# The first two sums of seven-product MLP units, written by an accumulating DMA instead of a VectorE add

## The reference

```python
m = rms_norm(h, mlp_norm[i])
h = h + jnp.square(jax.nn.relu(m @ w_mlp_up[i])) @ w_mlp_down[i]
```

## Time and profile before

| | us |
|---|---|
| median of 3 runs | 1630.5 |
| lowest and highest run | 1630.49, 1630.96 |
| span of the profiled execution | 1630.0 |
| TensorE busy | 1623.6 |
| VectorE busy | 1017.8 |
| ScalarE busy | 660.2 |
| GpSimd busy | 115.0 |

### The profile page before, as it was taken

How to read it: one execution, slowest core, us unless ns; L and a number is a source line. 1 busy time by engine, 2 the same in 40 slices (tenths; PEclk the granted TensorE clock), 3 DMA queues, 4 the chain that set the end, 5 groups by cost and what they waited for, 6 DMA issues and landing times.

```text
span 1630.0 us, 20189 instructions
## 1 busy us (share of the span) xinstructions
PE 1623.6 (100%) x8480; PEld 1345.9 (83%) x8480; DVE 1017.8 (62%) x1523; ACT 660.2 (41%) x919; POOL 115.0 (7%) x102
## 2 busy tenths in 40 slices
PE   9999999999999999999999999999999999999999
PEld 7877878898989888888888888877777888888887
DVE  6797664696756757576466357546655576366353
ACT  5476445354444446333122223456565333122221
POOL 1300000011111100000000000312101100000000
PEclk9999999999999999999999999999999999999999
DMA  5310228356454521222322313322221223222211
GB/s 187 109 46 27 104 78 121 82 115 136 87 135 86 161 84 72 79 102 104 107 100 100 107 59 124 101 94 87 76 77 52 78 104 111 98 102 98 109 59 71
DMA packets 28059, 156.01 MB, mean 96 GB/s; under 512 B 3712, under 2 KB 5392, under 8 KB 12096
## 3 DMA queue, kind: packets, MB, share of 16 engines
q1 hardware_dynamic: 26352, 149.75, 25.7%
q0 software_dynamic: 1328, 4.86, 5.5%
q10 hardware_dynamic: 288, 0.10, 0.0%
HBM read 149.98 MB, written 4.72 MB: 95 GB/s over the span
## 4 chain that ended last, share of the span: by engine, by line
PE 94%; DVE 3%; ACT 2%; DMA 1%; POOL 0%; issue 0%; SPq 0%; DVEq 0%; ACTq 0%
PE bank L725 23%; PE bank L726 23%; PE bank L727 23%; PE bank L731 3%; PE bank L733 3%; PE bank L732 3%; PE bank L1183 2%; PE bank L1185 2%; PE bank L1184 2%; PE bank L1421 1%; PE bank L980 1%; PE bank L1431 1%; PE bank L1447 1%; ACT WH L1490 1%; DMA RAW<-in_W 1%; PE bank L965 1%
## 5 line engine op out<-in xcount | busy, mean ns | idle before, releaser
L1913 DVE TENSOR_TENSOR WL<-RAW,WH 128x2048 fp32r<-128x2048 f32 (+2 forms) x122 | 273.0, 2243 | 193.5 <-ACT WH L1490 193.5
L725 PE MATMUL bank<-AH,WH 128*128 128x512 f32 (+1 forms) x974 | 382.9, 393 | 0.6 <-DVE WL L1963 0.4
L727 PE MATMUL bank<-AH,WL 128*128 128x512 f32 (+1 forms) x974 | 379.2, 389 | 0.0
L726 PE MATMUL bank<-AL,WH 128*128 128x512 f32 (+1 forms) x974 | 379.1, 389 | 0.0
L1490 ACT ACTIVATE WH<-RAW 128x2048 fp32r<-128x2048 f32 (+2 forms) x122 | 227.0, 1867 | 174.3 <-PE bank L727 138.0
L725 PE MATMUL bank<-HH,WH 128*128 128x512 f32 x608 | 236.6, 389 | 0.0
L726 PE MATMUL bank<-HL,WH 128*128 128x512 f32 x608 | 236.6, 389 | 0.0
L727 PE MATMUL bank<-HH,WL 128*128 128x512 f32 x608 | 236.5, 389 | 0.0
L725 PEld LDWEIGHTS bank<-AH,WH 128*128 128x128 f32 (+1 forms) x974 | 182.5, 187 | 42.4 <-issue 2.4
L727 PEld LDWEIGHTS bank<-AH,WL 128*128 128x128 f32 (+1 forms) x974 | 182.4, 187 | 38.7
L726 PEld LDWEIGHTS bank<-AL,WH 128*128 128x128 f32 (+1 forms) x974 | 182.5, 187 | 38.3 <-issue 1.0
(11 more groups left out here) (347 smaller groups left out, 2378.9 us busy)
## 6 DMA issues: line engine op xcount, KB each, us to landing
RAW<-in_W SPq DMA_DIRECT2D x124, 1024.0 KB, 4.8
RAW<-in_W SPq DMA_DIRECT2D x9, 768.0 KB, 4.2
X<-in_XT SPq DMA_DIRECT2D x16, 256.0 KB, 5.4
ev_scratch<-ev POOLq DMA_DIRECT2D x16, 160.0 KB, 7.6
Gb<-ev_scratch SPq DMA_DIRECT2D x16, 128.0 KB, 3.0
Gb<-ev_scratch SPq DMA_DIRECT2D x16, 112.0 KB, 2.7
out<-X SPq DMA_DIRECT2D x7, 256.0 KB, 2.0
RAW<-in_W SPq DMA_DIRECT2D x2, 512.0 KB, 5.6
```

The lines of the kernel that those rows point to most:

```text
L725: e.matmul(o, a, h, start=first, stop=False)
L726: e.matmul(o, a, l, start=False, stop=False)
L727: return e.matmul(o, c, h, start=False, stop=last)
L1913: e.tensor_tensor(k.WL[j][:, 0:n], k.RAW[RAW_OF[u]][:, 0:n], k.WH[j][:, 0:n].bitcast(F), SUB).then_inc(*WLO.mark(u))
```

## The change

Seven of the eleven fast units (up7, 8, 9, 11, 12, 13, 15: all but up5, and but the second of each run) no longer make "s1" on VectorE. SP writes block 3 of the unit's weights twice into `stage[0:2]`, from memory, once stageB of the fast unit before has been split, and adds 16 to `sums_seeded`. POOL waits for that and issues a DMA that adds blocks 0 and 1, again read from memory, to `stage[0:2]`; its landing adds 16 to `sums_added`. VectorE waits for this and goes on with "s2" and "s4". POOL's issue stands at "mid" of the unit two before, or, for up9 and up13, at the first down step of the group of four ahead. SP's seed stands right behind the unit's own load.

```diff
+def fast_before(u):
+
+    return max((v for v in FAST if v < u), default=0)
+
+
+SEEDED = [u for u in sorted(FAST) if fast_before(u) and (u - 1 not in FAST or u - 2 in FAST)]
...
+    k.seeded, k.summed = semaphore("sums_seeded"), semaphore("sums_added")
...
     def added(u):
 
         raw = k.RAW[RAW_OF[u]][:, :].rearrange("p (c n) -> p c n", c=4)
-        before = max((v for v in FAST if v < u), default=0)
-        w.wait_ge(loaded(k, u), WLO("stageB", before) if before else DVE("tl", 3))
-        e.tensor_tensor(k.stage[:, 0:2, :], raw[:, 0:2, :], raw[:, 3:4, :].to_broadcast([P, 2, QUARTER]), ADD).then_inc(
-            *DVE.mark("s1", u))
-        w.wait_ge(DVE("s1", u))
+        before = fast_before(u)
+        if u in SEEDED:
+            w.wait_ge(loaded(k, u), (k.summed, 16 * (SEEDED.index(u) + 1)))
+        else:
+            w.wait_ge(loaded(k, u), WLO("stageB", before) if before else DVE("tl", 3))
+            e.tensor_tensor(k.stage[:, 0:2, :], raw[:, 0:2, :], raw[:, 3:4, :].to_broadcast([P, 2, QUARTER]), ADD).then_inc(
+                *DVE.mark("s1", u))
+            w.wait_ge(DVE("s1", u))
...
+    def add_blocks(u):
+
+        w.wait_ge((k.seeded, 16 * (SEEDED.index(u) + 1)))
+        e.dma_start(k.stage[:, 0:2, :], k.W[u, :, 0:2 * QUARTER].rearrange("p (i n) -> p i n", i=2), accum_op=ADD).then_inc(k.summed, 16)
+
     for step, *x in mlp_order():
+        if step == "mid" and x[0] + 2 in SEEDED:
+            add_blocks(x[0] + 2)
+        elif step == "down" and x[1] == 0 and UNIT["down", 4 * x[0] + 3] + 1 in SEEDED:
+            add_blocks(UNIT["down", 4 * x[0] + 3] + 1)
...
     for u in range(3, attention + 4):
         load(u)
+        if u in SEEDED:
+            w.wait_ge(WLO("stageB", fast_before(u)))
+            e.dma_start(k.stage[:, 0:2, :], k.W[u, :, None, 3 * QUARTER:4 * QUARTER].to_broadcast([P, 2, QUARTER])).then_inc(k.seeded, 16)
```

## The result

| | before | after |
|---|---|---|
| median of 3 runs, us | 1630.5 | 1666.1 |
| lowest and highest, us | 1630.49, 1630.96 | 1665.13, 1667.03 |
| span of the profiled execution, us | 1630.0 | 1663.3 |

The ratio is 1.0219, with a 95% interval of 1.0201 to 1.0238: 35.6 us slower. 1651.5 was forecast, with a range of 1639 to 1672.

What follows compares the result with a forecast made beforehand. TensorE, busy 1623.6 of 1630.0 us, was taken as the bound, so the adds were worth 0; loop stalls of 19.3 us plus 1.7 for the clock made 21.0: 1651.0 profiled, 1651.5 as a median, range 1639 to 1672.

Steps and rivals of the forecast that it cites:

- What bounds the kernel: TensorE, busy 1623.6 of 1630.0 us, never waits for VectorE; taking the adds off VectorE is worth 0.
- Rival 3: Faster: VectorE's 8.5 us less work would free TensorE somewhere; at best 1630 us, chance 0.02.
- The loop: Through one buffer, stage: D + 6.6 us per unit against TensorE's 9.84; stalls sum to 19.3 us.
- Rival 1: Quick transfers: both DMAs land in about 3.0 us, D near 6.0, 3.6 us lost, 1634; chance 0.08 of under 1639.
- D: Time from stageB of the unit before to the landing of the sums: 9.7 us, ends 7.7 and 12.9.
- 512 KB should land in 3.6: SP's seed of stage, sized by the slope between loads of 1024 and 768 KB: 3.6 us, at least 3.0.
- The accumulate without a load: POOL's accumulating DMA into stage: 4.6 us as pe_x plus 1.2 for the extra read, 5.8; bounds 4.6 and 9.0.
- Rival 2: Slow accumulate: at 12 us D = 15.9, stalls 50.3 us, time 1684; chance 0.10 of over 1672.
- VectorE's part of the loop: VectorE's steps from the end of the add to the end of stageB: 6.57 us, taken as 6.6.
- The clock term: TensorE falls to half clock at one of the long stalls (up8, up12): 1.7 us, ends 0 and 3.4.
- up9 and up13: At these units 14 us hide a load of 4.8 and a D of 9.7, so the stall is 0.
- The margin of 0.4 us behind up8: First down split comes 8.04 us behind stageB of up8, TensorE needs it after 8.43; loss 0, but not by much.

Runs made afterwards that it cites:

- e_no_add: The kernel before without the add of 128x1024 in all eleven units, nothing in its place (output wrong): 1630.3 us, ratio 1.0004.
- e_two_buffers: The kernel after with a second buffer for the first two sums of up7, up11 and up15, all DMA bytes kept: 1630.8 us, ratio 1.0004.
- e_filled: The kernel after with useless products ahead of product a of up7, 8, 11, 12 and 15, keeping TensorE busy: 1664.6 us.
- e_load_later: The kernel after with SP's load behind the seed (up7, 8, 11, 12, 15) held until the sums have landed: 1653.5 us, ratio 1.0142.
- e_plain_second: e_load_later with POOL's DMA as a plain copy instead of an accumulate: 1647.4 us in one run.
- e_load_first: The kernel after with SP's load of the next unit issued ahead of the seed (up7, 8, 11, 12, 15): 1659.4 us, ratio 1.0178.
- e_covered: The kernel after with only up9 and up13 seeded, the other five making their sums on VectorE: 1630.4 us, ratio 0.9998.
- e_wide_seed: e_load_later with the seed reading blocks 2 and 3 in runs of 4 KB (sums wrong): 1652.3 us in one run.
- e_scalar_seed: The kernel after with ScalarE seeding stage by a copy of block 3 from RAW instead of SP's DMA: 1640.2 us, ratio 1.0055.

## Why the prediction was right, and where its size was off

**What bounds the kernel** held: without the add, and without any DMA in its place, the time is the same (e_no_add, 0.9995 to 1.0013). Rival 3, faster, falls with it.

**The loop** held, in its place, its order and its formula: the same bytes outside the loop cost about 1.5 us (e_two_buffers), and TensorE waits in just up7, 8, 11, 12 and 15, released by VectorE. It does so at "a" in all five, but at "c" only in up11 and up15: in up7, 8 and 12, where the prediction had waits at both, "a" ran at half clock and ended just as stageB did. Rival 1, quick transfers, fell by the landings: 5.9 and 7.1 us, not 3.0. Even the plain copy of 512 KB with no load beside it took 4.1, from POOL's queue. The Trainium skill (DMA: Bandwidth & Descriptors, Anatomy of one DMA) has 2.0 us plus bytes over 436 GB/s, an estimate of 3.2 us for it; page and measurement differ, and the measurement decides. (The D = 6.7 of rival 1 took this estimate, which is for GpSimd's DMAs, for SP's seed as well.)

**D was mis-sized**, 9.7 instead of 13.3, worth 17.8 us, of which VectorE's part (below) took some 2.5 back; that is the gap between 21.0 and 35.6 us. The term "512 KB should land in 3.6" measured 5.9. The slope between loads of 1024 and 768 KB was carried down to 512 KB of 2 KB runs, which took 4.5 alone, and I let the load issued 0.4 us behind the seed cost nothing, where it cost 1.4. The page before had a row of this very size and queue, which was passed over:

```profile
RAW<-in_W SPq DMA_DIRECT2D x2, 512.0 KB, 5.6
```

These two were issued 5.0 and 6.4 us into the span, among other loads. With 5.6 for the seed, D would have been 11.7 and the sum 29.3 us.

The prediction had named the load behind the seed as SP's next instruction, and said that it would land 4.8 us after its issue and have "little left" when the accumulate came. In the kernel after it took 7.8 (345.78 to 353.60 in up7), so it was still under way 2.1 us after the accumulate's issue at 351.49, and cost that one 1.1 us. The Trainium skill (DMA: Bandwidth & Descriptors, Issuing engines are not separate DMA queues) says that all DMAs run on the same 16 engines and interleave, whoever issued them; the trace agrees, 4.5 us alone and 5.9 in company for SP's seed, 5.9 and 7.0 for POOL's accumulate beside SP's load.

The accumulate without a load measured 5.9, where the prediction had 5.8; that is partly luck, since its copy was quicker (4.1, not the 4.6 of pe_x) and its add dearer (1.8, not 1.2). Nor was pe_x alone, as rival 1 has it: a scratch write was under way beside it, and BC and a load were issued while it ran.

The range held because of its upper end, 35.3 us for D = 12.9. That it comes so near the measured 35.6 is luck too: it was made of a seed of 3.6 and an accumulate of 9.0, and measured were 5.9 and 7.0. Rival 2, at 12 us for the accumulate, was too far.

**VectorE's part of the loop** was 0.5 us shorter than the 6.6 taken from before, five times 0.5 = 2.5 us the other way: 5 times 3.56 more in D is 17.8, less 2.5 is 15.3, and 19.3 + 15.3 = 34.6, against 34.5 measured at the c's.

**The clock term** of 1.7 was right in size: 1.5 us from c to the down products, and 1.5 by e_filled. It was right for a partly wrong reason. The clock fell at up7, 8, 12 and 15 (the first matmul of "a" or "c" there lasts 0.58 us, against 0.39 behind the wait at up11), not at one unit; most of each lay under a wait that was there anyway. The prediction's own row shows no idle time ahead of the fall, but 3.46 us of 3.46 busy, part of it with tiny products; a fall behind standing still is shown only by the stalls of the changed kernels.

**up9 and up13** were nought as said, though not by the cover computed: 4.8 + 9.7 is already more than 14, and D took 15.1 us at up9. VectorE waited 3.2 and 3.9 us there in the kernel after, and TensorE did not. **The margin of 0.4 us behind up8** held: the first down product had no wait.

## What to carry to other kernels

Before an operation is moved off an engine that isn't the bound, ask what the moved form puts into a loop with one buffer: two DMAs, one waiting for the other, put two full landings (here 5.9 and 7.0 us for 512 KB each) into every turn. Here a second buffer for every other unit hid them, and so did the lead of some 14 us at up9 and up13. Price a DMA in such a loop with whatever its queue issues right behind it, and an accumulating one above a copy. Look for the row of that size and queue before a slope is drawn through others. If the engine that sets the end never waits, expect no gain, and one kernel that leaves the operation out shows it.

## What the runs showed of the hardware

- An accumulating DMA of 512 KB into SBUF landed 5.9 us after its issue (mean of the five in e_load_later, 5.5 to 6.6), the same DMA as a copy after 4.1 us (e_plain_second), and the accumulate beside a load of 1 MB after 7.0 (the kernel after).
- 512 KB written in 2 KB runs landed in 4.5 us alone, in 5.9 us with 1 MB issued right behind it on the same queue, and in 5.7 (4.9 to 7.7) with that load 1.8 us or so ahead. The load of 1 MB, usually 4.8 us, took 7.8 behind such a seed.
- The profile of the kernel before has a stretch at half clock near 190 us. The granted clock from 187 to 200 us was 0.87 there and in e_load_later and e_load_first, 1.00 in the kernel after, in e_two_buffers, e_covered, e_filled, e_no_add and e_wide_seed, and 0.74 in e_plain_second and e_scalar_seed, though that part of the program is the same in all. At half of 3.41 us each, this is a scatter of 0, 1.7 or 3.4 us that has nothing to do with the change. The runs without a trace fit it: of 21 runs of the kernel before, those with a granted clock of 1.000 over the whole took 1629.1 us in the median, those with 0.999 took 1630.8, and those with 0.998 took 1632.7.
